# Gating the last eight experts' rows before the weighted sum, with the residual added in PSUM

## The reference, cut to what matters

```python
# T = 256 tokens, 8 heads, 16 experts chosen per token and head, D = 1024, float32
u  = take(expert_u, idx)                       # rows of U
vv = take(expert_v, idx)                       # rows of V
a  = gelu(einsum("td,thk->thk", h, u))         # one dot product per token and expert
y  = einsum("thk,thkd->td", g * a, vv)         # weighted sum of 128 rows per token
x  = x + gate * y                              # gate: one vector of 1024, the same for all tokens
# then rmsnorm(x) * gain (+ shift): the input of the next layer, or the output
```

## Time and profile before

| | |
|---|---|
| median of 3 runs | 2337.32 us (2336.9 to 2343.87) |
| the profiled execution's own time | 2334.75 us |
| its span on the core | 2333.1 us |
| busy share | PE 90%, DVE 69%, ACT 35%, POOL 24% |
| mean granted TensorE clock | 0.967 |
| first experts stage, from its first gather to its last weighted sum | about 822 to 1480 us |
| second experts stage, likewise | about 1668 to 2325 us |

### The profile page before, as it was taken

The page is one execution under the profiler, slowest core; times in us unless marked ns, Lnnn a source line. Parts: engine busy times, 40 slices in busy tenths (PEclk is TensorE's granted clock), DMA queues, the critical chain, the costliest instruction groups (busy, mean ns, idle before and its releaser), DMA issues.

```text
span 2333.1 us, 24987 instructions
## 1 busy us (share of the span) xinstructions
...
## 2 busy tenths in 40 slices
...
GB/s 292 73 323 332 336 123 108 205 355 334 276 209 145 198 313 422 421 421 422 421 422 421 422 421 421 334 181 156 252 397 422 421 421 421 421 421 421 421 422 300
DMA packets 162060, 772.82 MB, mean 331 GB/s; under 512 B 13688, under 2 KB 14072, under 8 KB 90271
## 3 DMA queue, kind: packets, MB, share of 16 engines
...
## 4 chain that ended last, share of the span: by engine, by line
DMA 30%; PE 28%; DVE 5%; issue 1%; ACT 1%; POOL 0%; DVEq 0%; POOLq 0%; ACTq 0%
DMA ring<-in_experts_uv_dram,experts_at 15%; DMA experts_v_slot<-in_experts_uv_dram,experts_at 10%; PE experts_first L3204 9%; PE experts_fourth L3204 8%; DMA experts_spare<-in_experts_uv_dram,experts_at 4%; PE experts_fourth L3185 2%; PE mix_sums L233 2%; PE mix_sums L234 1%; PE mix_sums L235 1%; PE experts_first L3158 1%; PE experts_second L3158 1%; PE experts_first L3185 1%; DMA experts_xn<-in_experts_uv_dram,experts_at 1%; DVE ring L2870 1%; DVE experts_v_slot L2870 1%
## 5 line engine op out<-in xcount | busy, mean ns | idle before, releaser
L3055 ACT ACTIVATE experts_diagonal<-ident,experts_weight 128x128 f32<-128x128 f32 x488 | 155.9, 390 | 633.8 <-DVE experts_weight L2925 623.5
L2671 POOL DMA_INDIRECT ring<-in_experts_uv_dram,experts_at x248 | 236.5, 954 | 357.7 <-PE experts_first L3204 192.8
L228 DVE TENSOR_TENSOR early_w_lo<-ring,early_w_hi 128x1024 fp32r<-128x1024 f32 x196 | 243.2, 1261 | 95.5 <-ACT early_w_hi L2321 52.7
L3204 PE MATMUL experts_first<-ring,experts_diagonal 128*128 128x512 f32 x560 | 263.3, 619 | 49.0 <-ACT experts_diagonal L3055 49.0
L3204 PE MATMUL experts_fourth<-ring,experts_diagonal 128*128 128x512 f32 x432 | 207.9, 630 | 47.1 <-ACT experts_diagonal L3055 47.1
L2870 DVE CUSTOM_DVE_ANT_0 ring<-ring,experts_third 128x1024 f32<-128x1024 f32 x140 | 170.6, 1218 | 100.2 <-DMA ring<-in_experts_uv_dram,experts_at 99.2
L3204 PE MATMUL experts_fourth<-experts_v_slot,experts_diagonal 128*128 128x512 f32 x368 | 184.1, 646 | 38.6 <-ACT experts_diagonal L3055 36.6
L3204 PEld LDWEIGHTS experts_first<-ring,experts_diagonal 128*128 128x128 f32 x560 | 107.8, 197 | 186.3 <-issue 124.9
L2870 DVE CUSTOM_DVE_ANT_0 ring<-ring,experts_second 128x1024 f32<-128x1024 f32 x108 | 131.8, 1221 | 89.3 <-DMA ring<-in_experts_uv_dram,experts_at 87.8
L3204 PEld LDWEIGHTS experts_fourth<-ring,experts_diagonal 128*128 128x128 f32 x432 | 85.2, 202 | 166.3 <-issue 107.0
L2870 DVE CUSTOM_DVE_ANT_0 experts_v_slot<-experts_v_slot,experts_second 128x1024 f32<-128x1024 f32 x92 | 112.3, 1221 | 87.0 <-DMA experts_v_slot<-in_experts_uv_dram,experts_at 86.9
...
## 6 DMA issues: line engine op xcount, KB each, us to landing
...
```

Source lines behind the costliest of these rows:

```text
L228: return dve.tensor_tensor(out_lo, a, hi.bitcast(F32), ALU.subtract)
L2671: pool.indirect_dma_start(pair(i), None, rows, bass.IndirectOffsetOnAxis(ap=at[:, n, j:j + 1], axis=0)).then_inc(pair_in[slot[i]], 16)
L3055: act.activation(diagonal[:, i % TOPK, :], K.ident[:], ACT.Copy, scale=weight[:, n, i % TOPK:i % TOPK + 1]).then_inc(diagonal_ready, 1)
L3204: mm = pe.matmul(y[n // PH][:, b, :], diagonal[:, j, :], v_row(i)[:, b * HALF:(b + 1) * HALF], start=n % PH == 0 and j == 0, stop=False, s ...
```

## The change

At the end of both stages the gate is applied to the V rows of the last eight steps (`GATED`, 248 to 255) instead of to their sum:

- POOL multiplies V rows by `factor2` in place, whole rows for steps 248 to 252, and only the second half of the columns for 253 to 255 (`SHARED`). It does so behind its last gather, each when its row has landed.
- DVE multiplies the first half of the columns for 253 to 255, each behind that step's weight.
- The sum up to step 247 stays in `fourth`. DVE multiplies it by the gate (`give_base`, two halves), behind steps 249 and 250, and first waits until PE has done step 247.
- PE adds into `first` (now called `ended`): x by a matmul with the identity ahead of step 246, the eight gated rows, and the gated sum by a matmul with the identity behind steps 250 and 251. In the last eight steps it takes the second half of the columns first (`ENDS`), and waits for the gated rows.
- `give_last` is gone. ACT squares straight from PSUM, and DVE multiplies PSUM by the gain. In layer 0 ACT copies the finished x back (`keep_last`). The first token half's splitting in layer 0 moves from steps 246 and 247 to 243 and 244, since `first` must be free by step 246.
- Two semaphores are joined into one (`first_given`), and the last 5 zero matmuls of layer 0 write another bank.

The hunks below stand in this order: names; POOL behind its last gather; DVE in `unit`; DVE behind the last step; ACT; PE in `weighted`.

```diff
+    GATED, SHARED = range(ALL - 8, ALL), range(ALL - 3, ALL)
+    ENDS = (1, 0)
+    ended = first
...
@@ -2699,6 +2703,11 @@
+        pool.wait_ge(row_in, 1)
+        for i in GATED:
+            f = part(ENDS[0]) if i in SHARED else slice(0, D)
+            pool.wait_ge(pair_in[slot[i]], pair_arrived(i))
+            pool.tensor_tensor(v_row(i)[:, f], v_row(i)[:, f], factor2[:, f], ALU.mult).then_inc(gated_pool, 1)
...
@@ -2881,6 +2890,11 @@
                 if i in SINGLES:
                     weigh_one(i)
+                if i in SHARED:
+                    f = part(ENDS[1])
+                    dve.tensor_tensor(v_row(i)[:, f], v_row(i)[:, f], factor2[:, f], ALU.mult).then_inc(dve_gated, 1)
+                if i in (GATED.start + 1, GATED.start + 2):
+                    give_base(i - GATED.start - 1)
...
-            elif (n, j) in ((LAST, 6), (LAST, 7)) and out is None:
+            elif (n, j) in ((LAST, 3), (LAST, 4)) and out is None:
...
-        def give_last(n):
...
+        def give_base(n):
+            dve.wait_ge(v_used, GATED.start)
+            dve.tensor_tensor(added[:, part(n)], y[1][:, n, :], factor2[:, part(n)], ALU.mult).then_inc(dve_gated, 1)
...
@@ -2969,14 +2981,15 @@
-        for n in range(2):
-            give_last(n)
         dve.wait_ge(last_squared, 2)
+        dve.tensor_tensor(gained[:, part(ENDS[0])], ended[:, ENDS[0], :], K.mod[:, 0, part(ENDS[0])],
+                          ALU.mult).then_inc(dve_gated, 1)
         dve.tensor_scalar(last_ms[:, 1:2], last_ssq[:, 1:2], 1.0 / D, EPS, ALU.mult,
                           ALU.add).then_inc(last_ms_done, 1)
-        dve.wait_ge(x_given, 3)
-        own.several(*(dve.tensor_tensor(gained[:, part(n)], K.x[:, 1, part(n)], K.mod[:, 0, part(n)], ALU.mult)
-                      for n in range(2)))
+        dve.wait_ge(last_squared, 3)
+        dve.tensor_tensor(gained[:, part(ENDS[1])], ended[:, ENDS[1], :], K.mod[:, 0, part(ENDS[1])],
+                          ALU.mult).then_inc(dve_gated, 1)
+        dve.wait_ge(dve_gated, 2 + len(SHARED) + 2)
...
@@ -3080,6 +3094,10 @@
+        def keep_last(n):
+            act.wait_ge(dve_gated, 2 + len(SHARED) + n + 1)
+            act.activation(K.x[:, 1, part(ENDS[n])], ended[:, ENDS[n], :], ACT.Copy).then_inc(x_given, 1)
...
-            act.wait_ge(x_given, n + 2)
-            act.activation(third[:, n, :], K.x[:, 1, part(n)], ACT.Square,
+            act.wait_ge(y_halves, n + 1)
+            act.activation(third[:, ENDS[n], :], ended[:, ENDS[n], :], ACT.Square,
...
@@ -3199,13 +3219,29 @@
+                if i == GATED.start - 2:
+                    pe.wait_ge(x_given, 1)
+                    if out is None:
+                        pe.wait_ge(last_lo, 2)
+                    for b in range(2):
+                        pe.matmul(ended[:, b, :], K.ident[:], K.x[:, 1, part(b)], start=True, stop=False,
+                                  skip_group_check=True)
                 pe.wait_ge(diagonal_ready, i + 1)
-                for b in range(2):
-                    mm = pe.matmul(y[n // PH][:, b, :], diagonal[:, j, :],
+                for b in ENDS if i in GATED else range(2):
+                    if i in GATED:
+                        own_half = i in SHARED and b == ENDS[1]
+                        pe.wait_ge(dve_gated if own_half else gated_pool,
+                                   3 + i - SHARED.start if own_half else 1 + i - GATED.start)
+                    mm = pe.matmul(ended[:, b, :] if i in GATED else y[n // PH][:, b, :], diagonal[:, j, :],
...
+                if i in (GATED.start + 2, GATED.start + 3):
+                    b = i - GATED.start - 2
+                    pe.wait_ge(dve_gated, b + 1)
+                    pe.matmul(ended[:, b, :], K.ident[:], added[:, part(b)], start=False, stop=False,
+                              skip_group_check=True)
```

26 lines of the change are left out of this document (13 added, 13 removed).

## The result

The changed kernel takes **2350.31 us** (median of 6 runs, 2348.32 to 2353.73), the kernel before 2337.32 (6 runs on the same chip, 2335.18 to 2343.87): a ratio of **1.005, 95% interval 1.0039 to 1.006**. It is 13 us slower, where 2341.9 and a range up to 2346.0 were forecast. The profiled execution took 2349.68 with a span of 2348.1, 15.0 more than the 2333.1 of before, at a mean granted clock of 0.965 (0.967 before).

What follows compares the result with a forecast made beforehand. Gathers bound each experts stage, so only what follows the last landing changes: 4.5 - 0.65 (first stage) + 2.2 - 1.4 (last) = +4.65 us on the median 2337.32, forecast 2341.9 us, range 2335.0 to 2346.0.

Steps and rivals of the forecast that it cites:

- What bounds the kernel: Mid-stage: a stage lasts as long as its gathers; the change touches only what follows the last landing, plus engines' lateness.
- The tail: Behind each stage's last step: shorter chain to the scaling, -1.4 us in the last stage, -0.65 in the first.
- The sum: All terms, 4.5 - 0.65 + 2.2 - 1.4 = +4.65 us, put on the median 2337.32 to give 2341.9.
- PE's added matmuls: Last steps: four matmuls, 3.44 us per stage; idle time covers 1.14 in the first, leaving +2.3, and all in the last.
- POOL's durations: Last eight steps: a whole-row product on POOL takes 2.45 us, just under the landing period, half a row 1.3.
- Rival 1: POOL behind its last gather: products above 2.48 us fall behind the landings; 2345.6, or 2347.1 at the worse price; chance 0.15.
- DVE beside POOL: Last steps: SBUF-only DVE operations wait for POOL's instruction, PSUM ones don't; step 255 +4.5 us first stage, +2.2 last.
- I take the wait to POOL's end: DVE's 128 x 1 weights beside POOL: each waits until the running product ends, at most 2.45 us.
- Rival 2: DVE's weights beside POOL: small weights don't wait, PE terms stand alone, +0.25 us, 2337.6; chance 0.2.
- rival 4: Chain behind the last step: not shortened, so the costs stand alone, +6.7 us, 2344.0; chance 0.05.
- Rival 3: First stage's last steps: PE is not behind, 2.6 us earlier, and nothing waits for POOL; -2.05 us, 2335.3; chance 0.1.
- signs named in advance: Both ends: POOL rows 2.45 and 1.3, weights up to 2 us, PE's last step 6.6 and 4.3 us behind landing.

Runs made afterwards that it cites:

- e3: The changed kernel without POOL's and DVE's products on V rows or PE's waits for them, so the last eight rows are added ungated; ratio 1.0 to the kernel before.
- e1: The changed kernel with POOL waiting for its own product behind each one, a gap of 0.08 us between products; ratio 1.0006 to the kernel before.
- e12: The changed kernel with the last gather held until row 248 has landed, so gather and products follow directly in both stages; ratio 1.0073 to the kernel before.
- e14: e12 with POOL waiting once for its own first product, a single gap behind row 248's product; ratio 1.0003 to the kernel before.
- e5: The changed kernel with POOL starting its first product (row 248) only when row 249 has landed too; ratio 1.0006 to the kernel before.
- e13: e12 with POOL waiting once, behind the last gather, for DVE's dot product of row 248, a wait that came to nothing; ratio 1.0074 to the kernel before.
- e16: e12 with POOL waiting behind the held gather until row 248's diagonal is made; ratio 1.0014 to the kernel before.
- e4: The kernel before plus POOL's eight whole-row products behind its last gather, PE waiting for each; ratio 1.0032; four of ten times form the upper group, 2349.5 to 2352.07.

## Why the prediction was wrong

**What bounds the kernel.** Right as far as it can be seen: the first stage's gathers take the same time (653.8), the last stage's differ by no more than from one execution to the next, and only what follows the last landing is the change's.

**The tail.** Right in place, too small in size. From PE's last load to the scaling 4.51 became 2.71, -1.80 where -1.4 was forecast. The end of ACT's second square came 1.74 us behind the last load, where the working puts it at 2.07 (2326.05, with the last load at 2323.98): the two squares with their reads lie 0.65 apart, not 0.79, because the second starts before the first one's read is over. In the first stage -0.79 arrived (5.32 to 4.53 from the last load to the turning), forecast -0.65.

**The sum.** 2337.32 and 4.65 make 2342.0, not 2341.9; nothing hangs on it.

**PE's added matmuls.** Forecast +2.3 in the first stage and 0.0 in the last; e3 measures +0.93 and 0.0. The 3.44 us of matmuls are there. What failed is the cover (the sum didn't count this term, since DVE's wait was longer): PE's distance behind the rows, read from one execution, moves from one to the next by as much as the term. e3's step 248 started 6.39 us behind its dot product with x's two matmuls already in front of it, before it was 6.34 without them, and in the changed kernel PE would have been free for it 8.1 behind (1467.69 against 1459.60).

**POOL's durations.** Right: 2.35 and 1.26, where 2.45 and 1.3 were taken. Rival 1's condition, a product over 2.48, didn't occur.

**DVE beside POOL.** Right where POOL is on time: weights up to 1.72, wide operations with a PSUM operand free (0.69), weights ending with POOL's product. The half rows come behind such weights and took 0.68, without a wait of their own. In the last stage the last step of PE started 3.99 us behind the landing (2339.73 against 2335.74), where 4.3 was forecast; the whole stage came out at +0.1, forecast +0.8.

**The step that failed** is "I take the wait to POOL's end", between bounds of "nothing" and "a whole POOL product, 2.45, wherever it is issued". The upper bound was wrong. I had put POOL's five whole rows of the first stage back to back ("starts row 248 at 1460.0"; it was 1460.93) and let each weight in at every product's end. Where POOL goes into such a row of products straight from a gather, the ends don't let DVE in: the wait runs to POOL's first gap, 12.62 us. PE's idle time and its half clock behind it follow from that. The forecast of +4.5 for the first stage's last step became +11.3 (14.37 against 3.06); of the shift at the mixer, 10.2 us, 8.7 vanish with e1's gaps (12.23), while the rest of the change stays as it is, and e12's 21.08 becomes 12.03 with e14's single gap.

The earlier trace rows could not have shown it: POOL's products there stand 0.08 us apart, and the DVE product of 2.91 got in at such a gap. That is e1's case. The Trainium skill (SBUF — State Buffer, "SBUF: two separate sides") states that whoever starts first has the shared ports "for the whole instruction". For a product that follows a pause the runs agree (0.98 and 0.92 above, 1.00 in e5); behind a gather they don't, since DVE is kept out over six instructions, and the measurement decides.

**Rivals.** Rival 1 had the right sign and the right pair of engines, but its mechanism, products longer than the landing period, didn't happen; its 2345.6 to 2347.1 was too low. Rival 2 (small weights don't wait) is refuted by every row above, rival 4 (no shorter chain) by the 1.80. Rival 3 (PE not behind) is half true: 0.93 in place of 2.3. Of the signs named in advance, POOL's rows, DVE's idle time ahead of the gated sum and the shorter end held; the weights "with up to 2 us" and the 6.6 us of PE's start did not (13.1: the load at 1490.11 against 1477.02).

**What stays open.** Why a gather in front makes the difference. One page would fit: the Trainium skill (GPSIMD Engine Reference, "2.1 Instruction dispatch") says that each of POOL's cores starts the next instruction as soon as it has done its share of the last. If a gather leaves the cores out of step, then products without a gap never end on all of them at once, and one gap brings them together. The weights that were held before the gather had ended (e12, e13, e14, against e16's first stage) would fit that as well: some of the cores would have begun the product by then. No run here separates the cores, so this is argued and not shown. Whether anything but a gather ahead of the products does the same was not tried. Nor was an execution of e4's upper group profiled; that those four had the gather late is likely and not seen.
